# Waits moved at the seams of a two-block transformer kernel: bias tile, score permissions, split waits, one root chain, a conv half

## The reference, cut to what matters

```
u = rmsnorm(x); proj = u @ w_in                      # block 1
ya = sliding_window_attention(qa, ka, va, sinks, rel_bias) @ w_proj_a
yb = (rmsnorm(gated_linear_attention(qb, kb, vb, log_a)) * silu(ob)) @ w_proj_b
h  = x + (sigmoid(gate_a) * ya + sigmoid(gate_b) * yb) @ w_out
h  = h + (silu(z @ w_ffn_gate) * (z @ w_ffn_up)) @ w_ffn_down, z = rmsnorm(h)
x2 = rmsnorm(h, norm_final_g); u2 = rmsnorm(x2, norm_g_2)          # block 2
conv   = (causal_depthwise_conv(cg * u) * bg * silu(cz)) @ w_conv_out
mla    = (latent attention, 16 heads, two heads a pair) * silu(mz) @ w_mla_out
memory = (attention over 256 memory tokens, 4 heads) * silu(ez) @ w_mem_out
out = x2 + (sigmoid(gc) * conv + sigmoid(gm) * mla + sigmoid(ge) * memory) @ w_o
```

## Time and profile before

| | us |
|---|---|
| median of 3 runs | 2663.33 (2659.15 to 2665.44) |
| profiled execution | 2661.63 |
| its span | 2659.9 |
| TensorE (PE) matmuls busy | 2573.5 (97%) |
| VectorE (DVE) busy | 1558.0 (59%) |
| ScalarE (ACT) busy | 1128.7 (42%) |
| HBM read | 459.60 MB, 175 GB/s over the span |
| mean granted TensorE clock | 0.991 |

### The profile page before, as it was taken

The page is one execution under the profiler, slowest core; times in us unless marked ns, Lnnn a source line. Parts: engine busy times, 40 slices in busy tenths (PEclk is TensorE's granted clock), DMA queues, the critical chain, the costliest instruction groups (busy, mean ns, idle before and its releaser), DMA issues.

```text
span 2659.9 us, 30759 instructions
## 1 busy us (share of the span) xinstructions
PE 2573.5 (97%) x11745; PEld 2110.5 (79%) x11745; DVE 1558.0 (59%) x2168; ACT 1128.7 (42%) x1407; POOL 0.2 (0%) x4
## 2 busy tenths in 40 slices
PE   5999988999999999999999999999999999999999
PEld 3777666888888888888888878888887888878887
DVE  5566555456656565556656664566556666564554
ACT  3344422444444444443455444433343555444443
POOL 0000000000000000000000000000000000000000
PEclk9999999999999999999999999999999999999999
DMA  5845434655566666665655555554664555455654
GB/s 188 227 155 153 128 103 137 196 186 185 184 219 187 185 184 184 194 186 178 204 193 194 199 160 173 174 176 150 203 189 144 168 161 163 150 161 171 201 186 136
DMA packets 235301, 466.67 MB, mean 175 GB/s; under 512 B 19051, under 2 KB 27537, under 8 KB 234530
## 3 DMA queue, kind: packets, MB, share of 16 engines
q1 hardware_dynamic: 231296, 457.89, 54.9%
q10 hardware_dynamic: 3874, 7.01, 1.4%
HBM read 459.60 MB, written 5.24 MB: 175 GB/s over the span
## 4 chain that ended last, share of the span: by engine, by line
PE 66%; DVE 3%; ACT 1%; issue 0%; DVEq 0%; ACTq 0%
PE acc L445 18%; PE acc L447 18%; PE acc L446 18%; PE banks L579 2%; PE banks L785 2%; PE banks L784 2%; PE banks L786 1%; PE acc L784 1%; PE acc L785 1%; PE acc L786 1%; DVE w_lo L1471 1%; PE banks L935 1%; PE banks L934 1%; ACT w_hi L1084 0%; PE banks L953 0%
## 5 line engine op out<-in xcount | busy, mean ns | idle before, releaser
L1471 DVE TENSOR_TENSOR w_lo<-raw,w_hi 128x1024 fp32r<-128x1024 f32 (+1 forms) x866 | 1043.1, 1218 | 878.0 <-ACT w_hi L1084 855.5
L1084 ACT ACTIVATE w_hi<-raw 128x1024 fp32r<-128x1024 f32 (+1 forms) x866 | 906.8, 1055 | 1191.0 <-PE acc L447 1056.4
L445 PE MATMUL acc<-w_hi,x_hi_A 128*128 128x512 f32 x1880 | 749.1, 398 | 17.3 <-DVE w_lo L1471 12.2
L447 PE MATMUL acc<-w_hi,x_lo_A 128*128 128x512 f32 x1880 | 736.8, 392 | 0.0
L446 PE MATMUL acc<-w_lo,x_hi_A 128*128 128x512 f32 x1880 | 735.9, 391 | 0.0
L445 PE MATMUL acc<-w_hi,x_hi_B 128*128 128x512 f32 (+1 forms) x1216 | 475.5, 391 | 3.9 <-DVE w_lo L1471 3.9
L447 PE MATMUL acc<-w_hi,x_lo_B 128*128 128x512 f32 (+1 forms) x1216 | 471.6, 388 | 0.0
L446 PE MATMUL acc<-w_lo,x_hi_B 128*128 128x512 f32 (+1 forms) x1216 | 471.2, 387 | 0.0
L445 PEld LDWEIGHTS acc<-w_hi,x_hi_A 128*128 128x128 f32 x1880 | 355.8, 189 | 99.1 <-issue 20.2
L447 PEld LDWEIGHTS acc<-w_hi,x_lo_A 128*128 128x128 f32 x1880 | 355.3, 189 | 76.0
L446 PEld LDWEIGHTS acc<-w_lo,x_hi_A 128*128 128x128 f32 x1880 | 356.1, 189 | 72.1 <-issue 0.6
(11 more groups left out here) (265 smaller groups left out, 1337.2 us busy)
## 6 DMA issues: line engine op xcount, KB each, us to landing
raw<-in_w_in_dram SPq DMA_DIRECT2D x377, 512.0 KB, 4.0
raw<-in_w_ffn_gate_dram SPq DMA_DIRECT2D x88, 512.0 KB, 4.2
raw<-in_w_ffn_up_dram SPq DMA_DIRECT2D x88, 512.0 KB, 4.4
raw<-in_w_ffn_down_dram SPq DMA_DIRECT2D x88, 512.0 KB, 4.5
raw<-in_w_out_dram SPq DMA_DIRECT2D x32, 512.0 KB, 4.4
raw<-in_w_mem_kv_dram SPq DMA_DIRECT2D x32, 512.0 KB, 4.2
raw<-in_w_mla_out_dram SPq DMA_DIRECT2D x32, 512.0 KB, 3.8
raw<-in_w_o_dram SPq DMA_DIRECT2D x32, 512.0 KB, 4.8
```

What stands on the lines that cost most here:

```text
L445: mm(o, xh, hi[:, k, :], start=(kt == first_k), stop=False)
L447: last = mm(o, xl, hi[:, k, :], start=False, stop=(kt == (last_k or c.kts) - 1))
L1084: act.activation(w_hi[:, s, 0:n], raw[:, r, 0:n], ACT.Copy).then_inc(hi_done, 1)
L1471: dve.tensor_tensor(w_lo[:, s, 0:n], raw[:, r, 0:n], w_hi32[:, s, 0:n], ALU.subtract).then_inc(lo_done, 1)
```

## The change

Seven things move; no matmul is added or removed. The diff, cut to its core:

```
@@ places @@
-        cvT = work[:, 0:1024]
+        cvT = work[:, 0:1024], area(40, 4)
-        squares_at = [... for v in (work, area(40, 8))]
+        q_squares = work[:, 0:768]...
+        k_squares = work[:, 768:768 + 4 * DN]...
@@ SyncE @@
-                if name == "kva":
-                    sp.wait_ge(b_ready, 16)
-                    sp.dma_start(bias_t, shifted).then_inc(b_ready, 16)
@@ ScalarE, after the splits of kva and four of qb @@
             plain()
+            act.wait_ge(b_ready, 16)
+            act.dma_start(bias_t, shifted).then_inc(b_ready, 16)
             skip_units(4)
             W.background(7)
@@ TensorE: back() waits where the operand is read @@
                     if g == 0:
                         need(pe, acc_free[C.slot(2)], C.rounds(2))
+                        if c.name in late:
+                            late.remove(c.name)
+                            activations()
@@ TensorE, after the sliding window @@
-            activations()
+            late.append("proj_a")
             background("gate_a", "gate_a", "gate_a", "proj_a", "proj_a", "proj_a")
@@ TensorE, convolution: turns read cgt and bgt in the arena @@
-                unit(turn_pair)
-                unit(turn_pair)
+                turn_quarter(cgt)
@@ TensorE, MLA pairs @@
                 if turn:
-                    unit(turn_pair)
-                    unit(turn_pair)
+                    turn_quarter(side2)
+                    late.append("conv_out")
...
-                mla_pair(MLA_BACK[0], *chunks[o:o + 3], turn=(k == 0))
-                mla_pair(MLA_BACK[1], *chunks[o + 3:o + 7], wait=(k == 0))
+                mla_pair(MLA_BACK[0], *chunks[o:o + 3])
+                mla_pair(MLA_BACK[1], *chunks[o + 3:o + 7], turn=(k == 0))
@@ ScalarE, end of the convolution @@
-                gated()
+                if h == 0:
+                    gated()
+            W.split_next()
+            c = this()
+            W.ahead(1)
+            evac_tanh(c)
+            done_chunk(c)
+            W.ahead(1)
@@ ScalarE, MLA pair @@
-                if turn:
-                    W.ahead(2)
...
-                if turn:
+                if (i, pr) == (0, 1):
                     conv_split(1)
...
-                if (i, pr) != (1, 3):
-                    W.ahead(4)
+                W.ahead(4)
...
-            W.split_next()
             W.background(3)
@@ VectorE, sliding window @@
-                    dve.sem_inc(unit_src, 1)
-                    SRC.n += 1
-                    dve.sem_inc(unit_src, 1)
-                    SRC.n += 1
+                    if g == 0 and b == 0:
+                        dve.sem_inc(unit_src, 2)
+                        SRC.n += 2
...
-                    dve.sem_inc(unit_src, 1)
-                    SRC.n += 1
+                    more = 3 if b < T - 1 else 1
+                    dve.sem_inc(unit_src, more)
+                    SRC.n += more
                     W.back(SWA_BACK[g * T + b][2])
...
-                dve.sem_inc(unit_src, 1)
-                SRC.n += 1
+                more = 3 if g < AKV - 1 else 1
+                dve.sem_inc(unit_src, more)
+                SRC.n += more
                 low_part("B", 2 * g)
@@ VectorE, the root chain @@
-            row_end()
-            CP(r_final, sm[:, 2:4])
-            dve.tensor_reduce(sm[:, 0:2], sm[:, 12:20]...)
-            for _ in range(2):
-                TT(sm[:, 0:2], sm[:, 0:2], r_final, ALU.mult)
-            rsqrt(2, D)
-            TT(r_two, sm[:, 2:4], r_final, ALU.mult)
+            for k in range(2):
+                ins = dve.tensor_reduce(sm[:, 2 * k:2 * k + 2], sm[:, 4 + 8 * k:12 + 8 * k]...)
+            TS(sm[:, 20:22], sm[:, 0:2], 1.0 / D, EPS, ALU.mult, ALU.add)
+            dve.reciprocal(sm[:, 20:22], sm[:, 20:22])
+            TT(sm[:, 2:4], sm[:, 2:4], sm[:, 20:22], ALU.mult)
+            rsqrt(4, D)
+            first_ez = ALL[W.next - 1][0]
+            W.ahead(1)
+            CP(r_final, sm[:, 4:6])
+            TT(r_two, sm[:, 4:6], sm[:, 6:8], ALU.mult)
...
-                take_silu(ezs)
+                if h2 == 0:
+                    W.ahead(SPL - 1)
+                    take_silu(ezs, first_ez)
+                else:
+                    take_silu(ezs)
@@ VectorE, convolution @@
-                stage_pair(cgt)
+                dve.sem_inc(unit_src, 2)
+                SRC.n += 2
...
-                a = ask_tanh(this())
-                W.more()
+                c = this()
+                if h == 1:
+                    W.ahead(1)
+                a = ask_tanh(c)
+                if h == 0:
+                    W.more()
...
-                TT(bgt, bgt, etmp[:], ALU.mult)
-                stage_pair(bgt)
+                TT(side2 if h else bgt, bgt, etmp[:], ALU.mult)
+                if h == 0:
+                    dve.sem_inc(unit_src, 2)
+                    SRC.n += 2
+                else:
+                    W.ahead(1)
```

More of the change, by code:

```diff
@@ L335, in build @@
         rot = work[:, 12 * DN:12 * DN + 256].rearrange("p (k h n) -> p k h n", k=4, h=2)
-        squares_at = [(v[:, 0:768].rearrange("p (t n) -> p t n", t=T),
-                       v[:, 768:768 + 4 * DN].rearrange("p (t h n) -> p t h n", t=T, h=2)) for v in (work, area(40, 8))]
+        q_squares = work[:, 0:768].rearrange("p (t n) -> p t n", t=T)
+        k_squares = work[:, 768:768 + 4 * DN].rearrange("p (t h n) -> p t h n", t=T, h=2)
         rotated = area(6, 1).rearrange("p (t h n) -> p t h n", t=T, h=2)
@@ L414, in _ @@
                         body(i)
-                if name == "kva":
-                    sp.wait_ge(b_ready, 16)
-                    shifted = bass.AP(scratch.tensor, P - 1, [[BIASW, P], [P * (BIASW + 1), AH], [1, 2 * P]])
-                    sp.dma_start(bias_t, shifted).then_inc(b_ready, 16)
             for k in range(D // CW):
@@ L547, in background @@
                     behind.extend((c, g) for g in range(c.grans))
-            behind = []
+            behind, late = [], []
             def back(k):
@@ L879, in find, with with_pair @@
                 return next(c for c in singles if c.name == name)
-            def with_pair(name, at, more=None):
+            def with_pair(name, at, more=None, v=None):
                 c = find(name)
@@ L886, in with_pair @@
                     if g == at:
-                        unit(turn_pair)
-                        unit(turn_pair)
+                        if v is None:
+                            unit(turn_pair)
+                            unit(turn_pair)
+                        else:
+                            turn_quarter(v)
                         if more:
@@ L906, in _, with mla_pair @@
             n, chunks = next((n, cc) for nm, n, cc in SEG if nm == "mla")
-            def mla_pair(ks, uq, ukv, *others, turn=False, wait=False):
-                if wait:
-                    activations()
+            def mla_pair(ks, uq, ukv, *others, turn=False):
                 chunk(uq)
@@ L1196, in _ @@
             plain()
+            act.wait_ge(b_ready, 16)
+            shifted = bass.AP(scratch.tensor, P - 1, [[BIASW, P], [P * (BIASW + 1), AH], [1, 2 * P]])
+            act.dma_start(bias_t, shifted).then_inc(b_ready, 16)
             skip_units(4)
@@ L1403, in mla_pair @@
                 uq, ukv = mla_cc[(0, 3, 7, 10)[pr]:][:2]
-                turn = i == 0 and pr == 0
-                if turn:
-                    W.ahead(2)
                 W.background(1 + pr % 2, False, 2)
@@ L1409, in mla_pair @@
                 a = acc[W.C.slot(2)]
-                q_squares, k_squares = squares_at[turn]
                 act.activation(q_squares, a[:, :, 0:384], ACT.Square)
                 act.activation(qs, a[:, :, 0:384], ACT.Copy).then_inc(release(uq), 1)
-                if turn:
+                if (i, pr) == (0, 1):
                     conv_split(1)
@@ L2294, in conv_split @@
                 for p in range(2):
-                    y = cvT[:, p * 512:(p + 1) * 512]
+                    y = cvT[h][:, p * 512:(p + 1) * 512]
                     dve.wait_ge(unit_done, W.U.at(1))
@@ L2303, in conv_split @@
                     dve.wait_ge(unit_free, W.U.next())
-            def stage_pair(x):
-                for p in range(2):
-                    CP(stage[:, W.U.slot(4, p), :].rearrange("p (t n) -> p t n", t=T), x[:, :, p * 256:(p + 1) * 256]).then_inc(unit_src, 1)
-                    dve.wait_ge(unit_src, SRC.next())
             dve.memset(mask3[:, 1, :], 0.0)
@@ L2336, in conv_half @@
                         g = GCOL["conv_w_2"] + 8 * j + 4 * h + kt
[L2337 removed]
+                        y, v = cvT[h][:, kt * S:(kt + 1) * S], vT[:, kt, j:S + j]
                         if j == 0:
```

23 lines of the change are left out of this document (14 added, 9 removed).

## The result

The changed kernel takes **2638.62 us** (median of 4 runs, 2638.16 to 2642.11) against 2663.91 (4 runs, 2659.15 to 2665.44): ratio 0.9911, 95% interval 0.9894 to 0.9928. It is 25.3 us faster; the forecast was 2638.6, with 24.7 us of gain.

The account below looks back on a forecast made before the run. TensorE was busy 97% of the span, so only its waits at seams and the half-clock stretches behind them could be won. Seven terms summed to 24.7 us, giving 2638.6 us from a median of 2663.33, range 2630 to 2650.

Parts of the forecast that it names:

- A: Bias tile moved to ScalarE's queue, before the first scores: gain 1.5 us, bounds a loss of 8.6 to a gain of 6.5.
- B: Sliding-window scores told with the previous unit's turn: five of six waits go, gain 5.9 us, bounds 3.5 and 6.
- packet rule: Bias tile beside weights: queues move about equal packet numbers; the tile's 1 KB runs against 2 KB get a third.
- Rival 2: Bias tile served early and clock stays up behind the attention's end: gain 31.4 us, 2632 us; chance 0.13.
- rival 3: Bias tile starves beside the weights and the kernel is slower: 2670 us; chance 0.03.
- rival 1: Gains given back at VectorE's next in-order split, only some 13 us survive: 2650 us; chance 0.17.
- C1: End of the attention: its split awaited only where read, so the log-decay chain begins earlier; gain 3.2 us.
- C2: Linear-attention split awaited after `gate_b`: a 1.43 us wait for `w_lo` comes instead; gain 0.1 us, bounds 0 and 1.5.
- E: One VectorE chain for two roots: wait of 2.32 us and 1.6 of clock go; gain 3.9 us, bounds 2.3 and 4.
- D: Convolution's second half, `ukv` and first MLA pairs: waits and half clock go, 1.0 charged; gain 4.5 us, bounds 2 and 5.5.
- G: `gm` split before the last pair's end: wait of 3.80 us and half clock go; gain 5.6 us, bounds 3.8 and 5.6.
- Rival 4: Other waits merely take the places of those removed: 2662 us; chance 0.03.

Follow-up runs that it names:

- e1: Changed kernel with the bias tile back on SyncE's queue behind `kva`, ahead of the weights of `qb`: 2640.39 us, ratio 0.9904.
- e5: Kernel before the change, with only the sliding window's scores told with the turn: 2655.19 us, ratio 0.9965.
- set 2: Four kernels, each one part of the change alone on the kernel before: 2655.19, 2662.76, 2658.44 and 2658.45 us.
- e6: Kernel before the change, with only the single chain for two roots: 2662.76 us, ratio 0.9993.
- e8: Kernel before the change, with only the convolution's turns from the arena and its second split in MLA pair two: 2658.45 us, ratio 0.9983.
- e4: Changed kernel with the memory tile issued one feed-forward pass earlier: 2637.13 us, ratio 0.9896.
- e11: Changed kernel with bias tile in two transfers, memory tile earlier, log-decay halves together, heads' products told early, one split before an evacuation, memory's root later: 2616.61 us.
- e7: Kernel before the change, with only `gm`'s four granules split ahead of the last pair's end: 2658.44 us, ratio 0.9982.
- e10: Changed kernel with the linear attention's first two products of a head told with the previous head's turn: 2630.51 us, ratio 0.9877.
- e3: Changed kernel with the bias tile in two transfers, the first kv group's four heads first: 2632.65 us, ratio 0.9878.
- e2: Changed kernel with the bias tile issued six us earlier, behind `kva`'s last split: 2639.11 us.

## Why the prediction was right, point by point

The median was met to 0.02 us, which is luck; the terms show how much.

- **A, forecast 1.5, measured -0.1.** The offset goes from +0.81 at the turns of `kva` to +0.29 at the second unit's scores, 0.52 gained, of which B brings 0.62 (the first of its five waits, 0.46, and 0.16 that comes with each wait). Over more executions it is the same: this stretch took 36.6 and 36.9 us in e1 and e5, which have B and not A, and 36.6 to 37.0 in the six that have both and load the tile in one piece. The step that failed is the size of the tile's transfer: "(2.46 + 2.10) MB / 387 GB/s = 11.8 us, 123.8, with the signal 124.3". From 112 to 125 the two queues moved 2.63 + 2.06 MB at 361 GB/s, 13.0 us; the tile's last packets took another 1.2 us, and it landed 0.4 behind them, at 126.6. The two stretches, 112 to 125 and 125 to 126.6:

```profile
DMA packets 3401, 4.69 MB, mean 361 GB/s; under 512 B 103, under 2 KB 2119, under 8 KB 3401
...
DMA packets 35, 0.03 MB, mean 20 GB/s; under 512 B 3, under 2 KB 35, under 8 KB 35
```

The bytes were right to 0.13 MB. The rate was not: it was 379 GB/s before the tile joined in and 351 from 121.5 to 124, when the tile was nearly alone. And the forecast had a row that gave 2.9 us beside the bytes, placed 1.3 + 0.5 of them and put the other 1.1 at nothing without a reason; the slow tail of 1.2 is of that size. The tile's late first packet, at 114.3 and not 112, cost nothing in this sum, since the weights filled that time. The packet rule held, and the seam's place, its new wait (6.31 for 4.6) and its half clock came as said. Rival 2 (served early) falls with the landing and with e1; rival 3 (starved) never came near.
- **B, 5.9, measured 6.8** (+0.91 to -5.87), and 6.7 in e5. The term counted the waits in brackets; by the offsets each seam costs some 0.15 more. It counted no clock, and in the mean there is some: 8.0, as the table of set 2 has it. Nothing is late at the copies of the probabilities, so rival 1 falls here, and e6 to e8 say the same of the rest.
- **C1, 3.2, measured 3.4.** The chain of 11 us was named rightly as the next wait (3.03 against 3.02 in the earlier trace rows). The 1.7 for the clock is uncertain: the half clock that C1 was to remove follows the waits of 1.01 and 0.65 too. In the mean of five executions without C1 and nine with it, C1 is worth 2.4; the changed kernel's profile drew no loss there.
- **C2, 0.1, measured 0.** 1.43 for `w_lo`, as worked out. In e1 and e4 the half clock just before it lasted twice as long, 1.4 us more; whether C2 has a part in that is open. e11's single split ahead of the evacuation took that away too.
- **E, 3.9, measured 4.0** by offsets, 3.0 in the mean: its 1.6 for the clock was one draw of four.
- **D, 4.5, measured 5.4**, of which 1.68 is a clock that was lost in two executions of four; 4.6 in the mean. Both waits went. The charge of 1.0 for pair two was too high: 0.53 is left.
- **G, 5.6, measured 5.7**, and 5.7 in e7. The clock is lost here every time, and twice as long in two executions of four: 6.2 in the mean.
- **Left out: -1.1 for the memory tile.** In the two profiled executions it landed after 9.8 and 11.0 us, in others after 9.0 to 11.7; it is no effect of the change. The pass's own wait of 0.55 was in the trace of before, unread.

The sum of the measured terms is 24.1; the changed kernel's execution was 0.8 behind already at 110 us, before any part acts, which gives the 23.4 of the spans. A's shortfall of 1.6 and the memory tile's 1.1 were nearly made good by 0.9 each in B and D and 0.3 in the others. The medians are 2.0 further apart than the profiled pair, within their intervals, and that closed the rest. In the means the terms are -0.1, 8.0, 2.4, 0, 3.0, 4.6 and 6.2, 24.1 in all: the sum of 24.7 was nearly right because A's shortfall, and the clock that it priced too high at C1 and E, are made up by the clock that it left out at B and priced too low at G. Rival 4 (other waits take the place of those removed) falls with the list of waits. No case of the other sign came near, and the chances of 0.94, 0.03 and 0.03 were of the right kind.

## What to carry to other kernels

A permission that one engine gives another belongs to the last event that it truly depends on, not to the place where the order of work happens to put it: told with the event before, it took up to 1.9 us off every round of the attention (B), and 1.55 with a half-clock stretch behind it off every head of the linear attention (e10), and next to nothing gave it back (one new wait of 1.11). A transfer that is put beside a busy queue is to be sized by the bytes that share with it and by packets that alternate; to have it sooner, make it smaller or load the needed part first (e3: 6 us), since an earlier issue alone did nothing (e2). Price a seam's wait as certain and its half clock as a mean over several executions, and leave no seam out of the second: B's waits had no half clock behind them in the one profile that was read.

## What was unexpected of the hardware

- Behind most seams the loss to the clock, as worked out here, is 0, 1.68 or about 3.4 us, nothing between, with the same program and the same wait; waits of 0.55 to 1.74 us cost none in the feed-forward part (seven executions, and thirteen at the wait of 1.34), while 1.01 and 0.65 close together at the end of the attention cost some in six of nine.
- The bias tile on ScalarE's queue had its first packet 3.5 to 3.8 us behind the issue in seven executions. In the changed kernel its last 35 packets took 1.2 us, and it was taken as landed 0.4 us behind them. Ahead of the weights on SyncE's own queue the same tile took 8.3 us in all, 8.3 to 8.5 in six executions; beside them 15.9 to 16.2, and 21.8 when issued earlier.
- The same memory tile, at the same place, landed after 9.0 to 11.7 us. Why it varies is open: it was not tried.
